# One decoder step on one core: four gelu buffers, half of each U load issued by ScalarE, one DVE operation recast, V's first split moved

## The reference

```
s1,i1 = top16(q1 . keys1); s2,i2 = top16(q2 . keys2)      # per token and head, 8 heads, 128 keys each
top_s, j = top16(s1[a] + s2[b]); eid = i1*128 + i2        # 16 experts of 16384 per head
g   = softmax(top_s)
act = gelu(u[eid] . x)                                    # u: 16384 x 2048
out = sum over k of (g * act)[k] * v[eid[k]]              # v: 16384 x 2048
```

## Time and profile before

| | us |
|---|---|
| median of three runs | 3624.67 (3616.17 to 3635.93) |
| the profiled execution | 3626.37 |
| its span | 3624.6 |
| PE, PEld busy | 3244.1, 3005.2 |
| DVE, ACT, POOL busy | 1921.2, 1356.5, 1039.2 |
| U stage (128 blocks) | about 1930 to 2886 |
| V stage (128 blocks) | about 2898 to 3625 |

### The profile page before, as it was taken

The page is one execution under the profiler, slowest core; times in us unless marked ns, Lnnn a source line. Parts: engine busy times, 40 slices in busy tenths (PEclk is TensorE's granted clock), DMA queues, the critical chain, the costliest instruction groups (busy, mean ns, idle before and its releaser), DMA issues. The chain is left out here.

```text
span 3624.6 us, 53340 instructions
## 1 busy us (share of the span) xinstructions
PE 3244.1 (90%) x21256; PEld 3005.2 (83%) x21256; DVE 1921.2 (53%) x2438; ACT 1356.5 (37%) x1708; POOL 1039.2 (29%) x537
## 2 busy tenths in 40 slices
PE   7999997968879888599799989888897799999998
PEld 7999996757868877599699988888887788888886
DVE  5344443332311001564446888797788457677765
ACT  5322232113522233343334333365666333333332
POOL 0000000004522343000105878866665601111100
PEclk9999997658988798799899999999999999999999
DMA  6555542315444542466676888978887978788864
GB/s 202 178 166 166 164 162 89 109 63 169 142 166 138 176 130 77 147 204 202 171 139 156 188 207 197 216 193 244 232 217 201 288 276 306 298 322 296 305 236 151
DMA packets 446567, 696.65 MB, mean 192 GB/s; under 512 B 30205, under 2 KB 342813, under 8 KB 418878
## 3 DMA queue, kind: packets, MB, share of 16 engines
q1 hardware_dynamic: 433950, 621.47, 58.0%
q0 software_dynamic: 9216, 67.11, 4.8%
q10 hardware_dynamic: 3264, 6.29, 0.5%
HBM read 627.94 MB, written 63.70 MB: 191 GB/s over the span
## 5 line engine op out<-in xcount | busy, mean ns | idle before, releaser
L2419 POOL TENSOR_TENSOR peer_uT_low<-peer_uT,peer_uT_high 128x1024 fp32r<-128x1024 f32 x256 | 667.7, 2634 | 352.9 <-ACT peer_uT_high L2446 352.4
L961 POOL TENSOR_TENSOR gate_low<-gate_raw,gate_high 128x512 fp32r<-128x512 f32 x192 | 244.9, 1301 | 1174.3 <-ACT gate_high L917 1174.2
L2322 PE MATMUL banks<-x_high,peer_uT_high 128*128 128x256 f32 x2048 | 512.9, 291 | 26.6 <-ACT peer_uT_high L2446 20.6
L2323 PE MATMUL banks<-x_low,peer_uT_high 128*128 128x256 f32 x2048 | 505.6, 286 | 0.0
L2322 PEld LDWEIGHTS banks<-x_high,peer_uT_high 128*128 128x128 f32 x2048 | 401.8, 196 | 29.4 <-ACT peer_uT_high L2446 18.5
L2564 DVE STREAM_TRANSPOSE peer_uT<-peer_u 128x1024 f32<-128x1024 f32 x256 | 312.3, 1231 | 177.6 <-DMA peer_u<-in_peer_u_dram 141.7
L2323 PEld LDWEIGHTS banks<-x_low,peer_uT_high 128*128 128x128 f32 x2048 | 400.4, 195 | 0.0
L228 PE MATMUL banks<-x_high,win_high 128*128 128x288 f32 (+1 forms) x1312 | 349.1, 296 | 0.0
L229 PE MATMUL banks<-x_low,win_high 128*128 128x288 f32 (+1 forms) x1312 | 348.7, 295 | 0.0
L198 ACT ACTIVATE win_high<-win_raw 128x2048 fp32r<-128x2048 f32 x84 | 160.9, 1915 | 334.6 <-DVEq L191 329.3
L2327 PE MATMUL banks<-x_high,peer_uT_low 128*128 128x256 f32 x2048 | 267.8, 283 | 15.7 <-POOL peer_uT_low L2419 15.6
(11 more groups left out here) (377 smaller groups left out, 6969.2 us busy)
## 6 DMA issues: line engine op xcount, KB each, us to landing
peer_u<-in_peer_u_dram SPq DMA_DIRECT2D x512, 256.0 KB
win_raw<-in_w_in_dram SPq DMA_DIRECT2D x38, 2048.0 KB, 8.1
peer_u<-in_peer_v_dram SPq DMA_DIRECT2D x64, 1024.0 KB, 5.1
peer_area<-in_peer_v_dram SPq DMA_DIRECT2D x64, 1024.0 KB
gate_raw<-in_w_in_dram SPq DMA_DIRECT2D x96, 512.0 KB, 3.9
w_raw<-in_w_up_ret_dram SPq DMA_DIRECT2D x8, 2048.0 KB, 9.8
w_raw<-in_w_out_dram SPq DMA_DIRECT2D x8, 2048.0 KB, 8.3
w_raw<-in_peer_w_q_dram SPq DMA_DIRECT2D x32, 512.0 KB, 7.5
```

The lines of the kernel that those rows point to most:

```text
L961: pool.tensor_tensor(self.low[:, p % 2, c, :, :], self.raw[:, p % 4, :, c * P:(c + 1) * P], self.high[:, p % 2, c, :, :], ALU.subtract).th ...
L2322: pe.matmul(out, UH[:, c, k, :], XH[:, k, 0:DENSE], start=(k == 0), stop=False)
L2323: pe.matmul(out, UH[:, c, k, :], XL[:, k, 0:DENSE], start=False, stop=False)
L2419: pool.tensor_tensor(UL[:, m % 2, part, :], UT[:, m % 2, part, :], UH[:, m % 2, part, :], ALU.subtract).then_inc(low, 1)
```

## The change

Four edits in `peer`, and one of order. `GE` gets four buffers instead of two, so `gelu(m)` waits for the store of block m-4, and there are four semaphores for the stores. Of the four quadrant loads of U, SP issues 0 and 1 as before, and ACT issues 2 and 3: those of blocks 0 and 1 before anything else of its part, those of block m+2 right after the two operations of `high(m)`. In `hot_rows` the one-hot row times weight is a scalar_tensor_tensor whose second tensor is the weight, broadcast along the row, instead of a tensor_scalar with two scalars. `split_v(0)` is ahead of `gelu(127)`. At the start `high(0)` is ahead of `keep_scores(0)`.

```diff
-        GE = st.sb("gelu", [P, 2, DENSE])
+        GE = st.sb("gelu", [P, 4, DENSE])
-        ge_stored = st.sems("gelu_stored0", "gelu_stored1")
+        ge_stored = st.sems(*(f"gelu_stored{r}" for r in range(4)))
+        def load_quadrants(queue, m, quadrants):
+            for g in quadrants:
+                queue.dma_start(U_PARTS[32 * g:32 * g + 32, m % 2, :, :], u_in[g, m]).then_inc(u_loaded[m % 4], 16)
                 def load_u(m):
                     sp.wait_ge(turned, after(2 * (m - 2) + 2))
-                    for g in range(4):
-                        sp.dma_start(U_PARTS[32 * g:32 * g + 32, m % 2, :, :], u_in[g, m]).then_inc(u_loaded[m % 4], 16)
+                    load_quadrants(sp, m, (0, 1))
-                    for c in range(2):
-                        sp.wait_ge(ge_stored[c], after(16 * (i + 1)))
+                    for m in (2 * i, 2 * i + 1):
+                        sp.wait_ge(ge_stored[m % 4], after(16 * (m // 4) + 16))
-                    sp.dma_start(S["gelu"][m], GE[:, m % 2, :]).then_inc(ge_stored[m % 2], 16)
+                    sp.dma_start(S["gelu"][m], GE[:, m % 4, :]).then_inc(ge_stored[m % 4], 16)
                         act.activation(UH[:, m % 2, part, :], UT[:, m % 2, part, :], ACT.Copy).then_inc(uT_high, 1)
+                    if m + 2 < BLOCKS:
+                        load_quadrants(act, m + 2, (2, 3))
                 def gelu(m):
                     act.wait_ge(hidden_done, after(m + 1))
-                    act.wait_ge(ge_stored[m % 2], after(16 * (m // 2)))
-                    act.activation(GE[:, m % 2, :], PS[:, 4 + m % 2, 0:DENSE], ACT.Gelu).then_inc(gelu_ready, 1)
+                    act.wait_ge(ge_stored[m % 4], after(16 * (m // 4)))
+                    act.activation(GE[:, m % 4, :], PS[:, 4 + m % 2, 0:DENSE], ACT.Gelu).then_inc(gelu_ready, 1)
+                for m in range(2):
+                    load_quadrants(act, m, (2, 3))
                 stage(0)
...
+                high(0)
                 keep_scores(0)
-                high(0)
...
+                    if m == BLOCKS - 1:
+                        split_v(0)
                     gelu(m)
...
                 for n in range(BLOCKS):
-                    split_v(n)
+                    if n:
+                        split_v(n)
...
-                        ins = dve.tensor_scalar(FIRST[:, b, j, :], iota[:], SEL[:, 0, t:t + 1], SEL[:, 2, t:t + 1],
-                                                ALU.is_equal, ALU.mult)
+                        ins = dve.scalar_tensor_tensor(out=FIRST[:, b, j, :], in0=iota[:], scalar=SEL[:, 0, t:t + 1],
+                                                       in1=SEL[:, 2, t:t + 1].to_broadcast([P, P]), op0=ALU.is_equal, op1=ALU.mult)
```

More of the change, by code:

```diff
@@ L2492, in keep, with split_v @@
                                    PS[:, 6 + q % 2, :].rearrange("p (t i) -> p t i", t=4), ACT.Copy).then_inc(w_ready, 1)
+                def split_v(n):
+                    act.wait_ge(v_loaded[n % 4], after(16 * (n // 4) + 16))
+                    if n < 4:
+                        act.wait_ge(hidden_done, after(BLOCKS - 1 if n == 0 else BLOCKS))
+                    else:
+                        act.wait_ge(out_done, after(n - 3))
+                    act.activation(VH[n % 4], V[n % 4], ACT.Copy).then_inc(v_high, 1)
+                for m in range(2):
+                    load_quadrants(act, m, (2, 3))
                 stage(0)
```

## The result

The changed kernel takes 3590.36 us (median of 7 runs, 3582.31 to 3603.44) against 3624.67: ratio 0.9908, 95% interval 0.9888 to 0.9928. It is 34 us faster (33 by the ratio) where 68 were forecast: inside the range, faster as forecast, and half the size. Its profiled execution took 3597.29 us (span 3595.5).

The account below looks back on a forecast made before the run. It took PE as the bound, with the U stage's spread held by gelu store waits; 50 + 11 + 3 + 9 + 1 = 74 us off 3626.4 gave 3552, 3551 at the median, shaded by 6 to 3557; range 3515 to 3618.

Parts of the forecast that it names:

- Four gelu buffers, 50 us less in the spread: U stage, four ten-block stretches with the spread: gelu's store wait goes, 384.5 to 334 us, 50 less.
- loop of 17.1 us for two blocks: U stage spread: hot rows, gelu store landing, gelu, high, POOL and hot rows again, 8.6 us a block.
- 26 us from the stores of weights: U stage spread: part of the 50 us, from gelu stores no longer waited for among 1 MB weight stores.
- Rival (d): U stage: the gelu wait was hidden after all and what replaces it is as long; 3620 us, chance 0.06.
- Blocks 2 to 65, 11 us: First row of the U stage: 6.63 to 6.45 us a block, DMA bounding it, 424.3 to 413 us.
- The last nine blocks, 3 us: End of the U stage, 60.3 us: loads are short with DMA at 0.97; 3 us less.
- Quadrants by ACT, 0 us: U loads: SP issues two DMAs less a block, ACT two more at 0.50 us each; no gain by itself.
- Rival (c): U stage: ACT's half of U comes late and paces blocks 2 to 65; slower, 3670 us, chance 0.07.
- (b): U stage: ACT's issues, at 1.12 us each, or the DMA engines become the bound; 3600 us, chance 0.22.
- Two-tensor operation, 0: Hot rows in the U stage: the new operation still waits for POOL, so the change gives 0 us.
- rival (a): Hot rows: the two-tensor operation doesn't take the lock against POOL; a further 32 us, 3525 us, chance 0.13.
- V, 9 us: Start of V: with its first split earlier, V begins at 2888 instead of 2898; 9 us taken.

## Why the prediction was right on the side and wrong on the size

*Four gelu buffers, 50 us less in the spread: the step that failed.* Measured alone they make it 1 us longer, which is nothing clear of noise, and the changed kernel's 9 us come with the quadrants: they give 14 alone, and with SP loading all of U the spread takes 390.5. The prediction had built a loop of 17.1 us for two blocks through the gelu wait and found it near the measured period of 8.8 a block; from that it took the wait as the pace. But the last part of that loop was DVE's wait for POOL, and that is what the pace hangs on. The earlier trace rows had it: DVE busy 82.65 of 88.0 us, 87.53 of 96.5. I read that as an engine kept long by a stall, of which removing the stall upstream would cure part. Without the gelu wait DVE is busy as before (343.4 of 375.4 us), with its waits for POOL spread otherwise over hot rows and dots. With the hot rows out of SBUF the spread falls by 54 us in the kernel before and 46 in the changed one. The "26 us from the stores of weights" failed with it: with the buffers alone the last three stretches take 295.8 us, 296.5 before. The prediction's own mark for being wrong was met: over 9 us a block (9.4) without a gelu wait. Rival (d), that the wait was hidden, is what happened in the spread; it had a chance of 0.06. That 3590 lies in the stated range (3515 to 3618) is luck: it does so by the gain of a part that was priced at nothing. With SP loading all of U the time is 3618.52, near the 3620 of (d).

Two readings of the rows were off besides. The first row holds 65 blocks, so 6.53 us each and not 6.63. And the spread has 20 dots in 40 blocks, one in every second and not in every third.

*Blocks 2 to 65, 11 us: right* (9), but for another reason: buffers alone gave 3, which is noise, and the quadrants alone nothing; the two together gave the 9. The issue times fit: ACT's half is issued early only when ACT doesn't stand at gelu.

*The last nine blocks, 3 us: too little* (9.4). Alone, the buffers gave 5 and the quadrants 3.

*Quadrants by ACT, 0 us: wrong, and the best part.* The prediction had the 0.87 us of issues that SP is spared for each block and put them into no sum. Rival (c) was afraid for the later half and (b) for the issues. Neither came. ACT's `high` waits 203 us for DVE's turn, so it mostly follows the turn closely, and the half isn't late (1.33 us from turn to last issue, 1.81 with SP alone). And the issues run partly beside ACT's own work; ACT's timeline shows the second inside two activations:

```profile
2431.80 0.32 ACTq L2238 DMA_DIRECT2D peer_u<-in_peer_u_dram  x1
2431.97 1.05 ACT L2449 ACTIVATE peer_uT_high<-peer_uT 128x1024 fp32r<-128x1024 f32 x1
2432.14 0.52 ACTq L2238 DMA_DIRECT2D peer_u<-in_peer_u_dram  x1
2432.91 1.05 ACT L2449 ACTIVATE peer_uT_high<-peer_uT 128x1024 fp32r<-128x1024 f32 x1
```

The prediction weighed the rule of the Trainium skill (DMA: Bandwidth & Descriptors, Issuing engines are not separate DMA queues), that a second issuing engine saves sequencer time only, and concluded that this part gives nothing. The trace agrees with the rule in blocks 2 to 65: the last issue ends 0.48 us sooner and the load lands 0.43 us sooner. It was the conclusion that failed: with the loads in sooner, blocks 2 to 66 took 7 us less than with SP alone (415.4 against 422.8). The spread took 15 less. The DMA share was to rise, and it fell, from 0.88 to 0.81; for that, and for the sooner landing in the later blocks, no run has the cause.

*Two-tensor operation, 0: right*, and rival (a) is out: mean 806 ns, single ones up to 2.8 us. The rule of the Trainium skill (SBUF — State Buffer, Who interferes with whom) is that a second SBUF input, or a two-port mode, contends for the ports shared with GpSimd. Both forms from SBUF agree with it (868 and 858 ns in the mean), and so does an operation with its only large input in PSUM (400 ns). The bound given for a lock never met was 32 us; it is worth 46 (64 in the kernel before, by the ratio). The bound went from 8.2 us a block to PE's 7.4. Measured, the spread went from 9.4 to 329.5 / 40 = 8.2. Both ends were low, the first since I took the hot rows' waits for a cost beside the pace and not for the pace itself.

*V, 9 us: at most 5, and not shown to come from the change.* At the end of U:

```profile
2859.44 0.76 DVE L2714 TENSOR_TENSOR peer_area<-peer_area 128x256 f32<-128x256 f32 x2 [7.77 <-DMA peer_area<-peer_weights]
...
2876.94 0.76 DVE L2714 TENSOR_TENSOR peer_area<-peer_area 128x256 f32<-128x256 f32 x2 [10.40 <-DMA peer_area<-peer_weights]
```

```profile
2863.73 0.47 PE L2390 MATMUL banks<-peer_uT_high,peer_act_high 128*128 128x512 f32 x1 [1.78 <-DVE peer_uT_low L2728]
...
2881.23 0.77 PE L2390 MATMUL banks<-x_high 128*128 128x512 f32 x1 [4.73 <-DVE x_low L2728]
```

PE's first wait fell from 12.5 to 1.8 us; `load_weights(1)` was late as feared, and took 5 back. With the split behind gelu(127) again V is as short (731.7 against 733.5). And it took 733.5 to 735.3 in three kernels that have neither the buffers nor the early split (quadrants alone, two-tensor operation alone, and the kernel before with hot rows from PSUM), where PE's first wait was 8.2 to 9.7 us. So most of the 5 us lies in the one trace of the kernel before, and no part is shown to give them.

*The start, 1 us:* not told from nothing.

## What to carry to other kernels

A loop of waits that adds up to the measured period isn't yet the pace: look for a second loop of the same length, above all on an engine that is busy nearly all of that stretch (here 87 to 94%), and ask of its busy time how much is waiting inside operations. The cheapest proof is to remove the suspected wait alone, or the other one alone, as here with 0 and 54 us in the spread. Where VectorE's short operations wait for GpSimd's long ones, a constant input copied once to PSUM can be worth more than any order of the work: here 46 us against 34 for the whole change.

## What the runs showed of the hardware that was not expected

- 1 MB loads, two quadrants issued by SP and two by ACT, landed 0.4 us sooner than with all four by either engine alone (7.47 against 7.90 and 7.96). In blocks 2 to 65 all of it was issue time (1.33, 1.81 and 2.09 us to the end of the last issue). Over the whole stage two issuing engines were worth 23 to 28 us of the kernel's time. The DMA share of those blocks was lower, too: 415.4 us at 0.81 against 422.8 at 0.89 and 424.8 at 0.85.
- A DVE operation of 128 columns with one input from PSUM took 400 ns in the mean beside POOL's subtractions, 858 to 868 with its inputs in SBUF; the custom dot of 2048 columns took 2245 in the spread, with 2809 from SBUF there. Fewer such waits cleared most of the loss in the spread although POOL's own mean hardly moved (2683 to 2665 ns).
